# State-space layer of a two-block model: the rotated scan input is summed in a PSUM bank by two TensorE products, and the output products of both column halves are issued in turn

## What is computed

```python
a_r = exp(lam_re*dt)*cos(lam_im*dt);  a_i = exp(lam_re*dt)*sin(lam_im*dt)   # one decay per group, state
bu  = einsum('gnh,btgh->btgn', b, u)          # 64 groups, 64 states, 16 channels each (complex)
x   = scan over t of  x_t = a * x_{t-1} + bu_t
y   = einsum('ghn,btgn->btgh', c_re, x_r) - einsum('ghn,btgn->btgh', c_im, x_i)
y   = gelu(y + d*u);   ab = y @ w_glu;   h += a * sigmoid(b)
```

## Time and profile before

| what | value |
|---|---|
| median of 3 runs | 1949.72 us |
| lowest to highest | 1947.89 to 1951.7 us |
| the profiled execution, its own time | 1947.97 us |
| its span | 1946.2 us |
| TensorE matmul busy | 1895.1 us (97%) |
| weight loads busy | 1528.0 us (79%) |
| VectorE busy | 1229.4 us (63%) |
| ScalarE busy | 927.2 us (48%) |
| GpSimd busy | 336.9 us (17%) |
| DMA | 166.97 MB, mean 86 GB/s |

### The profile page before, as it was taken

The page is one execution under the profiler, slowest core; times in us unless marked ns, Lnnn a source line. Parts: engine busy times, 40 slices in busy tenths (PEclk is TensorE's granted clock), DMA queues, the critical chain, the costliest instruction groups (busy, mean ns, idle before and its releaser), DMA issues.

```text
span 1946.2 us, 26640 instructions
## 1 busy us (share of the span) xinstructions
PE 1895.1 (97%) x9236; PEld 1528.0 (79%) x9236; DVE 1229.4 (63%) x1827; ACT 927.2 (48%) x1576; POOL 336.9 (17%) x222
## 2 busy tenths in 40 slices
PE   5999999999999999999999999999999999999998
PEld 3778788888888766788888888788888887777776
DVE  8954443443449787543443449888767867677673
ACT  4864432332335576532232335466546553366673
POOL 6942100000045000200000042022122215000002
PEclk9999999999999999999999999999999999999999
DMA  5214233323332211233232332222222222222222
GB/s 207 48 30 130 93 94 96 95 96 97 97 98 87 86 34 55 85 96 95 95 96 96 96 97 87 91 76 74 76 87 76 75 68 86 87 66 66 66 76 76
DMA packets 54522, 166.97 MB, mean 86 GB/s; under 512 B 13216, under 2 KB 13344, under 8 KB 53920
## 3 DMA queue, kind: packets, MB, share of 16 engines
q1 hardware_dynamic: 54432, 165.78, 27.8%
HBM read 161.30 MB, written 2.10 MB: 84 GB/s over the span
## 4 chain that ended last, share of the span: by engine, by line
PE 81%; DVE 10%; ACT 4%; issue 2%; DMA 0%; DVEq 0%; ACTq 0%; SPq 0%
PE bank L183 14%; PE bank L185 14%; PE bank L184 14%; PE bank L1597 4%; PE bank L1598 4%; PE bank L1599 4%; PE bank L2252 2%; PE bank L2253 2%; PE bank L2254 2%; PE bank L1621 1%; PE bank L1623 1%; PE bank L1622 1%; DVE w_lo L203 1%; PE bank L1673 1%; PE bank L2354 1%
## 5 line engine op out<-in xcount | busy, mean ns | idle before, releaser
L203 DVE TENSOR_TENSOR w_lo<-raw,w_hi 128x1024 fp32r<-128x1024 f32 x286 | 359.4, 1256 | 428.5 <-ACT w_hi L195 426.4
L195 ACT ACTIVATE w_hi<-raw 128x1024 fp32r<-128x1024 f32 x289 | 305.0, 1056 | 382.8 <-DMA raw<-in_w_dram 382.7
L183 PE MATMUL bank<-x1h,w_hi 128*128 128x512 f32 x680 | 266.1, 391 | 0.1
L185 PE MATMUL bank<-x1h,w_lo 128*128 128x512 f32 x680 | 264.6, 389 | 0.0
L184 PE MATMUL bank<-x1l,w_hi 128*128 128x512 f32 x680 | 264.6, 389 | 0.0
L183 PE MATMUL bank<-x0h,w_hi 128*128 128x512 f32 x640 | 250.3, 391 | 0.0
L185 PE MATMUL bank<-x0h,w_lo 128*128 128x512 f32 x640 | 249.0, 389 | 0.0
L184 PE MATMUL bank<-x0l,w_hi 128*128 128x512 f32 x640 | 249.0, 389 | 0.0
L232 POOL TENSOR_TENSOR sq<-h 128x512 f32 x38 | 45.8, 1205 | 741.5 <-DVEq L974 659.4
L1597 PE MATMUL bank<-x1h,w_hi 128*128 128x512 f32 x384 | 152.7, 398 | 0.7 <-DVE w_lo L203 0.4
L1599 PE MATMUL bank<-x1h,w_lo 128*128 128x512 f32 x384 | 149.8, 390 | 0.0
(11 more groups left out here) (442 smaller groups left out, 3570.1 us busy)
## 6 DMA issues: line engine op xcount, KB each, us to landing
raw<-in_w_dram SPq DMA_DIRECT2D x289, 512.0 KB, 3.6
h<-in_xT_dram SPq DMA_DIRECT2D x1, 2048.0 KB, 12.9
Ur<-in_xu_dram SPq DMA_DIRECT2D x8, 256.0 KB, 2.8
out_dram<-h SPq DMA_DIRECT2D x8, 256.0 KB, 2.3
const<-in_const_dram SPq DMA_DIRECT2D x1, 1028.0 KB, 14.0
B_st<-in_B_dram SPq DMA_DIRECT2D x1, 1024.0 KB, 7.5
C_st<-in_C_dram SPq DMA_DIRECT2D x1, 1024.0 KB, 15.0
p_in<-in_pT_dram SPq DMA_DIRECT2D x1, 1024.0 KB, 4.8
```

The source lines that it names most:

```text
L183: e.matmul(b, w_hi[:, w, k], xh[:, k], start=(k == 0), stop=False)
L185: last = e.matmul(b, w_lo[:, w, k], xh[:, k], start=False, stop=(k == KT - 1))
L195: e.activation(w_hi[:, z], raw[:, z], ACT.Copy).then_inc(hi_split, 1)
L203: e.tensor_tensor(w_lo[:, z], raw[:, z], w_hi[:, z].bitcast(F32), ALU.subtract).then_inc(w_split, 1)
```

## The change

In `rotated` TensorE now makes the scan's input itself: one product with the identity brings pr1 into bank 3, a second one with `turn` adds J applied to pr2, and pr2 is now -S sin (in `Sx`), made by VectorE from bank 2. ScalarE's copy of S and VectorE's subtraction V go. VectorE makes pr1 and pr2 of block T in step T, in the new function `factors`, between the tables and the fractions of block T+1; before, they were made at the head of step T+1. In the output products the two column halves alternate, product by product, and both are reported at the end. The order of the parts of TensorE's step is not changed.

```diff
-        s5_states = Steps(sem("s5_states"), "pr1 pr2 V Z po1 po2 W", ahead=4)
+        s5_states = Steps(sem("s5_states"), "pr1 pr2 Z po1 po2 W", ahead=4)
-        s5_kept = Steps(sem("s5_kept"), "Sx", ahead=4)
...
-            def s_kept(t):
-                e.wait_ge(s5_sums.sem, s5_sums.at("S", t))
-                e.wait_ge(s5_js.sem, s5_js.at("JS", t - 2))
-                s5_kept.took("Sx", e.activation(Sx[:, t % 2], grid(bank[2]), ACT.Copy))
...
                 if 0 < T < NBLK:
-                    s_kept(T)
                     turned(T)
...
+            def factors(t):
+                z = t % 2
+                e.wait_ge(s5_sums.sem, s5_sums.at("S", t))
+                e.wait_ge(s5_angles.sem, s5_angles.at("cos", t))
+                e.wait_ge(s5_states.sem, s5_states.at("W", t - 1))
+                s5_states.took("pr1", tt(tA[:, :, :], grid(bank[2]), cosb[:, z], ALU.mult))
+                e.wait_ge(s5_js.sem, s5_js.at("JS", t - 1))
+                s5_states.took("pr2", stt(Sx[:, 0], grid(bank[2]), -1.0, sinb[:, z], ALU.mult, ALU.mult))
...
-                    e.wait_ge(s5_kept.sem, s5_kept.at("Sx", t))
-                    e.wait_ge(s5_angles.sem, s5_angles.at("cos", t))
-                    e.wait_ge(s5_states.sem, s5_states.at("W", q - 1))
-                    s5_states.took("pr1", tt(tA[:, :, :], grid(bank[2]), cosb[:, z], ALU.mult))
                     e.wait_ge(s5_js.sem, s5_js.at("JS", t))
-                    s5_states.took("pr2", tt(turned, turned, sinb[:, z], ALU.mult))
-                    n().took("V", tt(turned, tA[:, :, :], turned, ALU.subtract))
-                    e.wait_ge(s5_states.sem, s5_states.at("V", t))
                     e.wait_ge(s5_out.sem, s5_out.at("JZ", q - 1))
...
+                if T < NBLK:
+                    factors(T)
+                if 0 <= T + 1 < NBLK:
                     fractions(T + 1)
...
             def step_sums(q):
...
-                e.wait_ge(s5_kept.sem, s5_kept.at("Sx", q - 1))
-                e.wait_ge(s5_states.sem, s5_states.at("pr1", q - 1))
+                e.wait_ge(s5_states.sem, s5_states.at("pr2", q - 1))
...
             def rotated(q):
-                e.wait_ge(s5_kept.sem, s5_kept.at("Sx", q))
-                e.wait_ge(s5_states.sem, s5_states.at("W", q - 1))
-                s5_js.took("JS", e.matmul(bk[3], C("turn"), Sx[:, q % 2].rearrange("p g c -> p (g c)"), start=True, stop=True))
+                e.wait_ge(s5_states.sem, s5_states.at("pr1", q))
+                e.matmul(bk[3], C("ident"), tA[:, :, :].rearrange("p g c -> p (g c)"), start=True, stop=False)
+                e.wait_ge(s5_states.sem, s5_states.at("pr2", q))
+                s5_js.took("JS", e.matmul(bk[3], C("turn"), Sx[:, 0].rearrange("p g c -> p (g c)"), start=False, stop=True))
...
-                    for k in (1, 2):
-                        e.wait_ge(s5_y_kept.sem, s5_y_kept.at(f"Y{k}", q - 1))
-                        for g in range(4):
-                            gg = 4 * k - 4 + g
-                            o = ybank(k)[:, g * LANES:(g + 1) * LANES]
+                    e.wait_ge(s5_y_kept.sem, s5_y_kept.at("Y2", q - 1))
+                    for g in range(4):
+                        both = [(4 * k - 4 + g, ybank(k)[:, g * LANES:(g + 1) * LANES]) for k in (1, 2)]
+                        for gg, o in both:
                             e.matmul(o, Ub[:, z, gg], Tm[:, z, gg].rearrange("p s h -> p (s h)"), start=True, stop=False)
-                            last = e.matmul(o, Wb[:, gg], TC[:, q % 3, gg, 1:].rearrange("p s h -> p (s h)"), start=False, stop=True)
-                        s5_out.took(f"Y{k}", last)
+                        last = [e.matmul(o, Wb[:, gg], TC[:, q % 3, gg, 1:].rearrange("p s h -> p (s h)"), start=False, stop=True) for gg, o in both]
+                    s5_out.took("Y1", last[0])
+                    s5_out.took("Y2", last[1])
```

More of the change, by code:

```diff
@@ L498, in s5_scalar @@
             s = small
-            for counters in (s5_kept, s5_st_kept, s5_k_kept, s5_angles, s5_y_kept, s5_gelu):
+            for counters in (s5_st_kept, s5_k_kept, s5_angles, s5_y_kept, s5_gelu):
                 counters.open(e)
```

## The result

| kernel | median | lowest to highest | runs | the profiled span |
|---|---|---|---|---|
| before | 1950.71 us | 1947.89 to 1952.8 us | 4 | 1946.2 us |
| changed | 1964.71 us | 1964.57 to 1965.27 us | 4 | 1962.7 us |

The ratio is 1.0076, with a 95% interval of 1.006 to 1.0092: 14 us slower by the medians, whose quotient is 1.0072, inside the range and 4.8 us above the predicted time.

The account below looks back on a forecast made before the run. TensorE bounds the dense part; VectorE leads the state-space blocks. Rings of 13.33 us against 11.74, plus step 7, start the dense part at 140.5 instead of 130.34: 1949.72 + 10.2 = 1959.9 us, range 1951 to 1966.

Parts of the forecast that it names:

- the ring: Blocks 0 to 6, po2 to po2 through pr1, scan and JZ: 5.61 + 2.87 + 4.85 = 13.33 us a block against 11.74.
- signs of being wrong: Scans every 11.2 us, `transposed` not delayed behind `rotated`, po1 blocked beyond JZ, or granted clock of the stretch under 1.
- 3.7 us for po1: Range's upper end: po1 stalled by GpSimd's tables in six blocks, 0 to 3.7 us; the sum took 0.
- 2.4 for halves that do not overlap: Range's upper end: output products of blocks 6 and 7 without overlap, 2 x 1.21 us more.
- The clock: TensorE's granted clock in the block stretches: 1.00, the 2.4 GHz level, before the change; a fall was left to rival 3.
- rival 3: TensorE's clock falls after waits for pr1: up to 41 us over six blocks, in part 15 to 40, 1975 to 2000; chance 0.06.
- Block 0 and the end: po2 of block 0 stays at 44.27; po2 of block 6 at 124.25, dense part at 140.5 against 130.34.
- po1 blocked by GpSimd: VectorE's po1, two SBUF inputs, blocked by GpSimd's table: at worst 0.61 us over 4.85 a block; taken as 0, hidden by JZ.
- The halves in turn: 32 output products in 2.04 us instead of 3.25, saving 1.21; off the path in the middle blocks.
- rival 2: Column halves of the output products do not overlap; blocks 6 and 7 cost 2 x 1.21 more, 1962.3 us; chance 0.07.
- Rival 1: VectorE stays the bound, JZ in time: 11.2 us a block, 1944.5 or 1947.0 us; chances 0.08 faster, 0.10 same.
- Step 7: Last cosine ends at 128.88; block 6's outputs and YT precede the last JZ, 135.8, though the scan ended at 133.4.

## Why the prediction was right, and by how much its steps were off

The sign and the mechanism of the ring were right: work queued behind `rotated` turned a period set by VectorE's work into a ring through TensorE. The predicted 10.2 us became 16.4 in the profiled execution, and that sum can be taken apart.

That the time lies inside the range is partly luck. One of the prediction's own signs of being wrong came true: the granted clock of the stretch is under 1, 0.92. The upper end of the range was made of 3.7 us for po1 and 2.4 for halves that do not overlap; neither came, and 7.4 us of the clock, which the sum put at nothing, used their room.

- *The ring.* Predicted 13.33, measured 13.09 at full clock: po2 to pr1 5.49 (5.61 predicted), pr1 to the scan 2.76 (2.87), scan to po2 4.84 (4.85). The missing 0.12 lies between VectorE's instructions up to pr1; the 0.11 is mostly the second 512-column product, which behind another of its kind ends 1.02 after its start (L819 above) and not 1.12. Over six blocks this is 1.4 us less than forecast.
- *The clock: the term that was mis-sized.* The sum took it at 1.00 and left its fall to rival 3. It fell, in part. Three rings of 14.48 to 14.78 in place of 13.09 are 4.6 us; block 0, with a pair of 2.79 in place of 1.82, adds 1.0; step 7, with 3.61 in place of 1.82, adds 1.8. Together 7.4 us. Rival 3 had the place right (the wait for pr1, "about 2.6 us", measured 2.63) and the price wrong: it doubled all TensorE's work of the ring, and "in part" began at 15 us. The rows show the first transposes back at their old length (0.60 at 110.80, as at 83.04), so a fall costs one pair, 1.0 to 1.8 us. That price holds for this kernel; in the kernel before with the halves in turn the clock stayed low for 10.5 us once. With eight waits at risk the lower bound should have been one fall, not fifteen microseconds, and a case with a price of 1.5 to 10 us belonged into the forecast, since nothing spoke for the clock holding.
- *Block 0 and the end:* po2 of block 0 came 1.47 later than assumed, 0.5 more than the clock explains. Here the prediction left its own walk: it let po1 set this place at 44.27, though its scan of about 40.0 and its 4.85 from scan to po2 give 44.9, set by JZ. From po2 of block 6 to the dense part 17.80 against 16.25, of which the clock is 1.8. Sum: 10.2 - 1.4 + 7.4 + 0.5 - 0.25 = 16.4.
- *po1 blocked by GpSimd:* taken as hidden by JZ, and it was. It lasted up to 2.94 us and cost 0.07 us in one block of the trace (1965.09 us without it). The prediction had it as a property of the changed order only; it is worth up to 6 us as soon as JZ is early.
- *The halves in turn:* 32 instructions in 1.9 to 2.0 us, 2.04 predicted, so rival 2 is out. But "the gain lies off the path there" was too kind. Off the path an earlier end is not neutral: it moved GpSimd's tables onto po1 and left TensorE idle long enough for the lower clock. Alone it costs the kernel before 7 us; in the changed kernel taking it back gains 4.6 us in the middle blocks of the trace, loses 2.7 at the end, and shows nothing in the run times.
- *Rival 1,* that JZ would be in time: scan to JZ was 3.68, as walked. Shown wrong.
- *Step 7:* pr1 came 3.26 us late by the cosine, the outputs of block 6 and YT ahead of the last JZ, each as walked; undoing the order gave 2.25 us in the trace, where rival 1 had priced it at 2.5, and nothing that the run times show.

On the two pages drawn on. The rule of SBUF — State Buffer, Who interferes with whom, in the Trainium skill holds in each of these kernels where a row was read: po1 with both inputs in SBUF ended 0.55 to 0.57 us behind GpSimd's instruction, and was 0.70 us where that one was short. TensorE: Matmul & The Clock Gate of the Trainium skill, Why this matters for your kernels, warns of gaps between bursts of matmuls. The traces agree, and go beyond it: most of the gaps here are shorter than those the page has in mind. The clock fell in some blocks after waits for another engine of 1.39 to 3.79 us, and in none of the blocks where the wait was 0.72 to 1.27.

## What to carry to other kernels

Where four engines are nearly full, ask of each moved step what is queued behind it on its engine, and walk the ring that this closes; here the walk gave the period within 0.25 us, though the change removed work from the leading engine. Then ask what every engine does with the time it gains: a TensorE that is left idle some 1.4 to 3.8 us in each block can lose its clock for the next products, and a helper engine that starts earlier may meet the leading one at a shared access. A speed-up off the path should be put only where nothing after it can be moved; here that left the last blocks, and a gain too small to tell from the noise.

## What was not expected of the hardware

- TensorE's clock fell after a single wait in a stretch where it is busy for 79% of the time (89.05 of 113 us), in some blocks and not in others that look the same: neighbouring blocks of 13.1 and 14.7 us had waits of 2.64 and 2.71. What decides between them was not found. After 0.72 to 1.27 us it did not fall in blocks 1 to 6. The shortest wait with a fall behind it is this one, in the kernel with `rotated` between the transposes and the direct products; the rows of L867, the same instructions, show it at either level:

```profile
115.05 0.44 PE L866 MATMUL bank<-Tm,Ub 128*64 128x128 f32 x4 [1.39 <-DVE Wb L758]
115.31 0.39 PE L867 MATMUL bank<-TC,Wb 128*64 128x128 f32 x4
...
115.83 0.64 PE L867 MATMUL bank<-TC,Wb 128*64 128x128 f32 x4
```

- The fall moves the median and widens the runs: ten executions of one kernel between 1947.8 and 1956.1 us with mean clocks of 0.995 down to 0.989, where the kernel before stays between 1947.86 and 1950.4 in 21.
